# A hybrid decoder trunk on one core: the causal mask added by TensorE, one minimum and one transposed copy per pair of blocks, transposes two steps behind the scores

## What is computed

```python
def masked_softmax(s, mask):
    s = jnp.where(mask, s, NEG_INF)
    m = jnp.max(s, axis=-1, keepdims=True)
    e = jnp.where(mask, jnp.exp(s - m), 0.0)
    return e / jnp.maximum(jnp.sum(e, axis=-1, keepdims=True), 1e-30)
# mla, per block of 128 queries and head
s = q @ k.T * scale
p = masked_softmax(s, kpos <= qpos)
o = p @ v
# nsa: out = gate_c * o_c + gate_s * o_s + gate_w * o_w
# o_c attends to 31 compressed keys, o_s and o_w are causal attention over ks/vs and kw/vw
```

## Time and profile before

| what | value |
|---|---|
| median of 3 runs | 1374.83 us (1374.44 to 1375.63) |
| profiled execution, span from the first to the last instruction | 1373.5 us, 24997 instructions |
| PE busy | 1309.3 us, 95% |
| DVE busy | 993.8 us, 72% |
| ACT busy | 686.0 us, 50% |
| POOL busy | 131.8 us, 10% |
| chain that ended last | PE 81%, DVE 8%, issue 5%, DMA 3%, ACT 2% |

### The profile page before, as it was taken

The page is one execution under the profiler, slowest core; times in us unless marked ns, Lnnn a source line. Parts: engine busy times, 40 slices in busy tenths (PEclk is TensorE's granted clock), DMA queues, the critical chain, the costliest instruction groups (busy, mean ns, idle before and its releaser), DMA issues.

```text
span 1373.5 us, 24997 instructions
## 1 busy us (share of the span) xinstructions
PE 1309.3 (95%) x10313; PEld 817.6 (60%) x10313; DVE 993.8 (72%) x1611; ACT 686.0 (50%) x1042; POOL 131.8 (10%) x113
## 2 busy tenths in 40 slices
PE   7999899999999999999999999989999999999992
PEld 4347445444444444444356445559988988988981
DVE  6985797686650366334895797567888889989996
ACT  5244676253320232212245776347487677677672
POOL 0010420320000000031010100320400000000003
PEclk9999999999999999999999999999999999999996
DMA  8330685324320344003331100229899999999975
GB/s 308 112 104 16 231 293 173 138 98 179 138 92 0 116 160 168 0 16 134 138 93 32 31 1 1 78 80 366 331 368 386 333 349 396 369 367 383 368 296 200
DMA packets 39998, 255.69 MB, mean 186 GB/s; under 512 B 5626, under 2 KB 6650, under 8 KB 25418
## 3 DMA queue, kind: packets, MB, share of 16 engines
q1 hardware_dynamic: 30490, 220.20, 42.6%
q0 software_dynamic: 8960, 33.26, 7.3%
q10 hardware_dynamic: 432, 0.59, 0.1%
HBM read 218.28 MB, written 33.65 MB: 183 GB/s over the span
## 4 chain that ended last, share of the span: by engine, by line
PE 81%; DVE 8%; issue 5%; DMA 3%; ACT 2%; POOL 1%; SPq 0%; DVEq 0%; POOLq 0%; ACTq 0%
PE bank L1120 19%; PE bank L1121 19%; PE bank L1122 19%; PE bank L1341 3%; PE bank L1387 2%; PE bank L1357 2%; DVE bank L2111 2%; DVE arena L2134 2%; PE bank L681 1%; PE bank L683 1%; PE bank L682 1%; PE bank L673 1%; PE bank L672 1%; PE bank L671 1%; DMA expert_slots<-arena,row_index 1%
## 5 line engine op out<-in xcount | busy, mean ns | idle before, releaser
L931 DVE SCALAR_TENSOR_TENSOR arena<-arena 128x3072 f16<-128x3072 f32 x86 | 288.3, 3352 | 10.8 <-ACT arena L785 10.7
L785 ACT ACTIVATE arena<-arena 128x3072 f16<-128x3072 f32 x86 | 237.9, 2767 | 41.6 <-DMA arena<-in_ew 19.9
L1120 PE MATMUL bank<-arena 128*128 128x144 bf16 (+3 forms) x894 | 219.3, 264 | 6.8 <-DVE arena L931 2.9
L1121 PE MATMUL bank<-arena 128*128 128x144 f16 (+3 forms) x894 | 219.2, 264 | 0.0
L1122 PE MATMUL bank<-arena 128*128 128x144 bf16 (+3 forms) x894 | 219.2, 264 | 0.0
L1120 PE MATMUL bank<-hh,wring_hi 128*128 128x512 bf16 x352 | 133.9, 380 | 0.0
L1122 PE MATMUL bank<-hh,wring_lo 128*128 128x512 bf16 x352 | 133.7, 380 | 0.0
L1121 PE MATMUL bank<-hl,wring_hi 128*128 128x512 f16 x352 | 133.7, 380 | 0.0
L1122 PE MATMUL bank<-hh,arena 128*128 128x512 bf16 x338 | 128.1, 379 | 0.0
L1121 PE MATMUL bank<-hl,arena 128*128 128x512 f16 x338 | 128.1, 379 | 0.0
L1120 PE MATMUL bank<-hh,arena 128*128 128x512 bf16 x338 | 128.1, 379 | 0.0
(11 more groups left out here) (332 smaller groups left out, 2618.3 us busy)
## 6 DMA issues: line engine op xcount, KB each, us to landing
arena<-in_ew SPq DMA_DIRECT2D x86, 1536.0 KB, 9.1
arena<-in_dw SPq DMA_DIRECT2D x22, 1536.0 KB, 6.5
wstage<-in_w_chunk SPq DMA_DIRECT2D x44, 512.0 KB, 3.6
expert_results<-iota POOLq DMA_DIRECT2D x9, 2048.0 KB, 21.3
arena<-in_cmp_w SPq DMA_DIRECT2D x2, 2048.0 KB, 10.0
expert_slots<-iota POOLq DMA_DIRECT2D x5, 512.0 KB, 18.8
expert_results<-wstage SPq DMA_DIRECT2D x5, 512.0 KB
arena<-in_w_tok SPq DMA_DIRECT2D x2, 1096.0 KB, 7.3
```

The source lines that it names most:

```text
L785: act.activation(ew_hi_[:, G % EP, :], ew[:, G % ES, :], ACT.Copy, scale=SW).then_inc(M["hi_ready"], 1)
L931: dve.scalar_tensor_tensor(out=ew_lo_[:, G % EP, :], in0=ew[:, G % ES, :], scalar=SW, in1=ew_hi_[:, G % EP, :], op0=ALU.mult, op1=ALU.subt ...
L1120: pe.matmul(out, w_hi, x_hi, start=first, stop=False)
L1121: pe.matmul(out, w_hi, x_lo, start=False, stop=False)
```

## The change

1. **Mask by TensorE.** `causal` becomes a 128x128 block with 0 on and below the diagonal and +1e30 above, a bf16 copy `causalb` is made once by POOL, and after the two score products of a step PE adds it to the diagonal block of each with a product of the identity. For this the scores are computed negated (the scales of ks, kw and mla's q change sign), so that the minimum is what is sought. `s_mm` is signalled once a step, after both.
2. **One minimum per pair.** A single `tensor_reduce` over the two PSUM banks of a step takes both minima; nothing is written back to PSUM. `nmx` is signalled once a step, and ACT waits for it before both exponentials.
3. **Scale.** One reciprocal in place of two instructions; the gate is applied as a second per-row factor in `scaled` for nsa. The reciprocal of the gates (`ginv`) is gone.
4. **One transposed copy per pair.** PE signals `pt_mm` once a step, ACT copies both banks in one instruction, and `turn(g)` waits for the copy of step g − 1. The layout of the transposed rows changes with it.
5. **Distance.** PE runs `turn(g - 2)` and the values that go with it in place of `turn(g - 3)`; ACT likewise `turned(g - 2)`; `collect` comes one step earlier.

```diff
@@ set-up @@
-        causal = sb("causal", T)
+        causal = sb("causal", P)
+        causalb = sb("causalb", P // 2)[:, :].bitcast(BF16)
...
+        def turned_block(s, i):
+            return PT_[:, s, :, i:i + 3 * i + 1:3, :]
         def turned_row(s, ab, kb):
+            return PT_[:, s, ab, 4 * kb:3 * kb + TT, :].rearrange("p b c -> p (b c)")
...
@@ PE @@
-                        pe.matmul(score_bank[n % 4][:, 0:N], q, k, start=True,
-                                  stop=True).then_inc(*signal("s_mm", l, n))
+                        pe.matmul(score_bank[n % 4][:, 0:N], q, k, start=True, stop=False)
+                    for ab in range(2):
+                        mm = pe.matmul(score_bank[(2 * g + ab) % 4][:, i * P:N], identb, causalb, start=False, stop=True)
+                    mm.then_inc(*signal("s_mm", l, g))
...
                         pe.wait_ge(*ready("pn", l, n))
-                        if n >= 2:
-                            pe.wait_ge(*ready("pt", l, n - 2))
+                        if g >= 1 and ab == 0:
+                            pe.wait_ge(*ready("pt", l, g - 1))
...
-                for g in range(ND + 3):
+                for g in range(ND + 2):
                     if g < ND:
                         scores(g)
-                    if g >= 3:
-                        turn(g - 3)
-                        if g - 3 >= TT:
-                            values((g - 3) // TT - 1, (g - 3) % TT)
+                    if g >= 2:
+                        turn(g - 2)
+                        if g - 2 >= TT:
+                            values((g - 2) // TT - 1, (g - 2) % TT)
@@ ACT @@
+                    act.wait_ge(*ready("nmx", l, g))
                     for ab in range(2):
                         n, N, at = 2 * g + ab, (i + 1) * P, 2 * i + ab
-                        act.wait_ge(*ready("nmx", l, n))
...
-                    for ab in range(2):
-                        n = 2 * g + ab
-                        act.wait_ge(*ready("pt_mm", l, n))
-                        act.copy(turned_block(u % 2, ab, i),
-                                 turn_bank[n % 2][:, 0:(i + 1) * P].rearrange("p (k q) -> p k q", q=P)
-                                 ).then_inc(*signal("pt", l, n))
+                    act.wait_ge(*ready("pt_mm", l, g))
+                    act.copy(turned_block(u % 2, i),
+                             turn_pair[:, :, 0:(i + 1) * P].rearrange("p a (k q) -> p a k q", q=P)
+                             ).then_inc(*signal("pt", l, g))
@@ DVE @@
-                    block = score_bank[n % 4][:, 0:(i + 1) * P]
-                    dve.tensor_tensor_reduce(block, block, causal[:, T - (i + 1) * P:], -1.0, 3.0e38, ALU.add,
-                                             ALU.min, nmx[:, m:m + 1]).then_inc(*signal("nmx", l, n))
+                    i, m = g % TT, 2 * g % 8
+                    dve.wait_ge(*ready("s_mm", l, g))
+                    dve.tensor_reduce(nmx[:, m:m + 2], score_pair[g % 2][:, :, 0:(i + 1) * P], AX_X,
+                                      ALU.min).then_inc(*signal("nmx", l, g))
...
                     dve.wait_ge(*ready("p", l, 2 * g + 1))
-                    if kind == "nsa":
-                        link(dve.scalar_tensor_tensor(out=r, in0=total, scalar=1e-30, in1=ginv[:, i, c:c + 4:3, br],
-                                                      op0=ALU.max, op1=ALU.mult))
-                    else:
-                        link(dve.tensor_scalar(r, total, 1e-30, None, ALU.max))
-                    dve.reciprocal(r, r).then_inc(*signal("scale", l, g))
+                    dve.reciprocal(rsum[:, u % 2, 2 * i:2 * i + 2],
+                                   ssum[:, u % 2, 2 * i:2 * i + 2]).then_inc(*signal("scale", l, g))
...
+                    if kind == "nsa":
+                        gate_at = 2 * P + 3 * head_of(u, at % 2) + br
+                        ins = dve.tensor_scalar(v, v, rsum[:, u % 2, at:at + 1], vtok[:, i, gate_at:gate_at + 1],
+                                                ALU.mult, ALU.mult)
@@ POOL, at the start @@
+            pool.tensor_copy(causalb, causal[:, :]).then_inc(*signal("by_pool", "unit"))
```

More of the change, by code:

```diff
@@ L69 @@
 NEG = -1.0e30
+MASKED = 1.0e30
 SCALE_MLA = float(DQK) ** -0.5
@@ L211, in trunk @@
                               for v in (wring_hi_, wring_lo_))
-        ARENA = 34176
+        ARENA = 34528
         arena = sb("arena", ARENA)
@@ L242, in trunk @@
         wukv = room(2 * HEADS * HD).rearrange("p (v m) -> p v m", v=2)
-        PT_ = arena[:, used[0]:used[0] + 2 * 2 * NP_ + T]
+        PB = 3 * (TT - 1) + TT
+        PT_at = used[0]
+        PT_ = arena[:, PT_at:PT_at + 2 * 2 * PB * P].rearrange("p (s a b c) -> p s a b c", s=2, a=2, c=P)
         cw1_ = room(2 * LP * P)
@@ L249, in trunk @@
         wuq = room(2 * HEADS * UQ).rearrange("p (c m) -> p c m", c=2)
+        room(PT_at + 2 * 2 * PB * P - used[0])
         qh = room(HEADS * T).rearrange("p (h t) -> p h t", h=HEADS)
@@ L378, in trunk @@
         cmax = small[:, 108:109]
-        bank = [ctx.enter_context(nc.psum_tensor(f"bank{i}", [P, T], F32)) for i in range(8)]
+        banks = ctx.enter_context(nc.psum_tensor("bank", [P, 8 * T], F32))[:, :].rearrange("p (b t) -> p b t", b=8)
+        bank = [banks[:, i, :] for i in range(8)]
         RING = 8
         score_bank = [bank[2], bank[3], bank[0], bank[1]]
-        turn_bank = [bank[4], bank[5]]
+        score_pair = [banks[:, 2:4, :], banks[:, 0:2, :]]
+        turn_bank, turn_pair = [bank[4], bank[5]], banks[:, 4:6, :]
         out_bank = [bank[6], bank[7]]
@@ L1559, in uq @@
                     act.activation(qh[0:DQK, h, :], bank[ring_of[("uq", l, h)]][0:DQK, :], ACT.Copy,
-                                   scale=SCALE_MLA).then_inc(*signal("uq", l, h))
+                                   scale=-SCALE_MLA).then_inc(*signal("uq", l, h))
                 def uk(j):
@@ L1678, in _ @@
                         gelu_tanh(g - TANH_DUO)
-                    if g >= 3:
-                        turned(g - 3)
+                    if g >= 2:
+                        turned(g - 2)
                 if l == 0:
@@ L2007, in uq @@
                     link(dve.tensor_tensor(a, qh[rows, h, :], cos32[rows, :], ALU.mult))
-                    link(dve.scalar_tensor_tensor(out=tmp[rows, 3, :], in0=b[turned, :], scalar=SCALE_MLA,
+                    link(dve.scalar_tensor_tensor(out=tmp[rows, 3, :], in0=b[turned, :], scalar=-SCALE_MLA,
                                                   in1=sin32[turned, :], op0=ALU.mult, op1=ALU.mult))
@@ L2067, in cmp_probs @@
                                       ALU.mult).then_inc(*signal("cmp_row", "probs", l))
-                    dve.reciprocal(ginv, gates).then_inc(*signal("ginv", l))
                 def lru_scan(_):
@@ L2154, in _ @@
                         lru_finish(*divmod(g - FINISH_DUO, 4))
-                    if g >= 3 * TT - 1 and g % TT == TT - 1:
-                        collect((g + 1) // TT - 3)
+                    if g >= 3 * TT - 2 and g % TT == TT - 2:
+                        collect((g + 2) // TT - 3)
                 collect(NU - 2)
@@ L2517, in tables @@
     t["byrank"] = np.tile(np.r_[NE - 1 - e, e, CAPS, RANK_AT].astype(np.float32), (P, 1))
-    t["causal"] = np.zeros((P, T), np.float32)
-    t["causal"][:, T - P:] = np.where(r[None, :] <= r[:, None], 0.0, NEG)
+    t["causal"] = np.where(r[None, :] <= r[:, None], 0.0, MASKED).astype(np.float32)
     end = np.arange(NCMP) * CMP_STRIDE + CMP_LEN - 1
```

39 lines of the change are left out of this document (11 added, 28 removed).

## The result

The changed kernel takes 1566.74 us (median of 4 runs, 1555.38 to 1582.91) against 1374.63 us: a ratio of 1.1366, with a 95% interval of 1.1307 to 1.1424. The ratio and its interval leave out the longest run, 1582.91 us, which counts as a slow one (the two medians as they stand divide to 1.1398). The kernel is slower by 192 us. I had forecast 1481, slower by 106, with a range of 1458 to 1520: the right direction and place, but too small.

A forecast was written before the change was run, and what follows sets the result against it. PE, busy nearly all the span, was taken to bound the kernel; with PE and DVE taking turns, the two attention loops grow by 52.7 and 53.8 us, together 106.5, from a median of 1374.83 to 1481 us; range 1458 to 1520.

The forecast's parts named there:

- The taking of turns: Attention loops: at distance two PE and DVE no longer overlap, a step lasts the sum of both parts; +106.5 us, chance 0.88.
- The chain's terms: Attention unit: scores and mask, minimum, reciprocal, scale and transposes, values; 15.6 us an nsa unit, 17.4 an mla unit.
- I take full clock, since gaps of up to 1.7 us are there now: Attention loops: TensorE's clock stays at 1.00 despite gaps of one to two microseconds in each step; no time added.
- the first rival: Attention loops: the clock falls and PE's column time doubles; 117 us if it lasts, 1598 us in all; chance 0.08.
- The rule against the change: TensorE in the attention loops: brief idling between groups of matmuls can swing it between full and half clock, losing throughput.
- It costs nothing: ACT's single copy, waiting for both heads' transposes, is hidden by a turn of three to five microseconds; only 0.1 us at the end.
- the clock case: Attention loops: TensorE's clock falls; 1598 us if it lasts, 1540 for half the time; chance 0.08, left out of the range.
- the full-clock case: Attention loops: the engines take turns with TensorE at full clock; 1481 us, bounds 1467 and 1516, chance 0.88.

The follow-up runs named there:

- e3_spares: The changed kernel with products of no use added in PE's wait for the scaled block, from the second unit on: 1491.84 us, ratio 1.0831.

## Why the prediction was right and wrong

- **The taking of turns: right.** It was read from the two queues, and the trace shows it in 34 of 36 steps; the distance alone accounts for 169 us on the new code and 164 on the old.
- **The chain's terms: right.** Scores to minimum 0.74, 0.95, 1.17, 1.38 us at full clock where I had 0.72, 0.93, 1.15, 1.36; minima of 0.42, 0.69, 0.96, 1.23 as summed from SBUF rows, so PSUM as a source costs nothing extra here; from reciprocal to scale 0.19. The scale of an nsa pair with its second factor takes 0.74 for 256 keys, 0.12 more than in the earlier trace rows. A loop at full clock is 151.7 against 150.4. That this is so close is in part luck: in `e3_spares` a whole nsa unit with its opening takes 16.9 us (865.74 to 882.63) and an mla unit 17.2 (932.77 to 949.94), some 0.25 less than summed, because the reciprocal starts before the minimum's modelled end (0.34 us after its start, where the minimum lasts 0.42), and the start and the end of the loop take some 3.5 us more than summed.
- **"I take full clock, since gaps of up to 1.7 us are there now": wrong,** and this is the step that failed. It set the term to zero in the sum and to 0.08 as a chance. It went by the length of the single longest gap, but the old loop had such gaps here and there (23 waits of a loop in which PE was busy 91% of the time), while the new one has one in nearly every step. I had even written that PE would be used less than in any full-clock stretch, and then put it aside. The clock is worth 75 us between medians (1566.74 less 1491.84), of the 86 by which the forecast was short; the other 11 are `e3_spares` above 1481, with layer 0's low clock at the start in them. So the first rival is what happened: its price was 117 us for loops wholly at half clock, and at the measured 70% of the time that makes roughly 82. The two profiled executions, from which the 70% and the full clock are read, are 91 us apart (1581.0 less 1490.3).
- **The rule against the change: right, against the row that I set above it.** TensorE was at 1.00 before and at 0.64 and 0.66 in the new loops, with PE moving from bank to bank between waits of at most 2.1 us. The Trainium skill (TensorE: Matmul & The Clock Gate, "A second HAM failure mode: psum-queue depth-cycling") names such brief idling between groups as a cause of a clock that swings between its levels. The trace agrees with the swing (0.61 and then 0.96 in the windows of 4 us from 880.00 in layer 1); its gaps here are waits for DVE. The rule should have outweighed my reading of one row.
- **"It costs nothing" of ACT's single copy: right at distance two as built, wrong beyond.** In the changed kernel, where a whole turn lies between, PE's transposes wait for the copy for only 0.4 us, in two waits. As soon as the turn-taking is gone its place costs 24 us.
- **The range** reached 1520 and left the clock case outside. It was built from the bounds of the full-clock case alone, and another case is what came.

## What to carry to other kernels

In kernels whose engines run fixed queues, write down for one step what each engine does in order, and look for an item that is ready but stands behind a wait for something just issued: there the engines take turns and the step becomes the sum of their parts. The cure can be to put the older item first, in both queues, rather than to change the distance or shave instructions; here that was worth 191 us at distance two and 5.6 us on a kernel already tuned. If a forecast tears regular gaps into TensorE's stream, price the lower clock as part of the forecast and not as a remote case, even when no single gap is much longer than those of before (2.1 us against 1.7 here).

## What was not expected of the hardware

- The granted clock fell to 0.50 after stretches in which PE was busy for 2.45 and 1.95 of 4 us, and stayed low through one in which it was busy for 3.40 of 4 us at the lower level. In `e3_spares` it held at 1.00 through two windows with PE busy for 2.27 and 1.95 of 4 us, so how busy PE is does not tell by itself where it falls. With products of no use in the waits, 1.0 to 1.7 us a step, layer 1's loop stayed at 1.00 and was 47 us shorter.
- How much of the time the clock is down differs between executions of the same program: 1555 to 1583 us for the changed kernel, 1490 to 1493 with the waits filled.
- A minimum over two PSUM banks at once costs what a reduction of the same count costs from SBUF: 1.04 ns an element and 0.15 us fixed.
